# Two attentions of a three-block transformer kernel: when the first two output weight units are split, where the first maximum stands, and thirteen filler products

## The chip, the cores and the metric

The kernel runs on one core of one Trainium2 chip. The metric is the device time of one execution in microseconds. All times below are microseconds unless a column says ns. PE is TensorE (matrix products; PEld is its weight load), ACT is ScalarE, DVE is VectorE, POOL is GpSimd, SP the queue that issues most transfers.

## The reference

A sequence of 256 tokens of width 1024 goes through a first block (a recurrent mixer, a sparse attention, a feed-forward network) and a second block of two layers. Only the attentions of the second block are touched:

```
for layer in range(2):
    h = rmsnorm(x, attn_norm[layer])
    x = x + (even_mixer if layer == 0 else mla_mixer)(h)
    h = rmsnorm(x, ffn_norm[layer])
    x = x + (silu(h @ w_gate) * (h @ w_up)) @ w_down
even_mixer: 8 heads of stick-breaking attention (two sigmoids, a running product)
            and 8 heads of sliding-window softmax, concatenated, @ w_out
mla_mixer:  low-rank q, k, v for 16 heads, causal softmax, @ w_o
```

## The kernel before, in words

All weights stream through a ring of four slots, `ring`, in units of 1 MB (128 rows of 2048 floats). SP loads a unit when `unit_done` says that the unit four before it is used up. For the second block each unit is split before use: ACT writes `w_hi` (the high part) in two halves (`high_p`, line 1434, and `high_d`, line 1439), DVE writes `w_lo` (the rest) in two halves (`first_half`, line 1979, and `second_half`, line 1985), and PE makes three products for one: high by high, high by low, low by high. `w_hi` and `w_lo` hold two units, so a unit can be split once the unit two before it has been used.

Both attentions run through `heads_pipeline` on PE, as 19 steps s = 0 to 18, one head entering at each of the first 16. In step s PE makes the scores of head s (even attention: lines 1217 to 1221; MLA, the second: 1330 and 1331) into `ps[s % 2]`; then some products that are left over from the projections (`early`, as many as `rate` says, up to step 4; the even attention's last two query units, MLA's last value unit `mla_uv` and last query unit `mla_uq3`); from step 6 on a piece of the output projection (`fill`, `out_rows`, line 594); three transposes of the weights of head s - 2 (line 695); another piece of the output projection; and the product of head s - 3 with its values (lines 706 and 707). Pieces of the output projection go in the order of the contraction: the first 8 need output unit 0, the next 8 unit 1, and so on, so unit 0 is wanted at step 6 and unit 1 at step 10.

ACT, DVE and PE each have a fixed order of instructions, and a wait holds up all that stands behind it on the same engine. The order per step is: on ACT the nonlinearity of head s (even heads 0 to 7: sigmoids, lines 1795 and 1796; else the exponentials, 1450 and 1452, and the scaling of head s - 1, 1461 and 1462), the copy of the transposed weights `pT` (1804, the even attention's heads 0 to 7 only), in even steps from 4 on the high part of a pair of heads (`out_high`, 1468), then `out_weights`. On DVE: for head s the running product (2509, 2515) or the maximum (`softmax_max`, 2005 to 2012), the reciprocal of the sum of head s - 1, the copy of `pT` (2027, where ACT does not make it), in even steps from 4 on the low part of a pair (`out_low`, 2032), then `out_weights`. `ps[3]` takes the values of two heads; PE starts the next pair only after `out_low` has read it (`att_lo`). Steps 3 and 4 (MLA: 3 and 5) also take queries (1787 and 2497; 2576).

In MLA PE runs 13 products whose result nobody reads into `ps[3]` at the end of the early products of step 2 (`mla_idle`, `idle_products`, line 483). DVE splits `mla_uq3` (unit 8 of "mla") and then takes the first maximum.

Of the kernel before, what the change touches and what calls it, by code (L numbers as in the profile page):

```python
# [21 lines left out]
P = 128  # L22
# [5 lines left out]
H = D // HD  # L28
# [19 lines left out]
KEYS = P + S  # L48
# [8 lines left out]
U = {}  # L57
# [35 lines left out]
def build(nc, ins, out):  # L93
    weights, aux_d, const_d, small_d, rows_d, swbias_d, x_d, pos_d = ins
    with ExitStack() as ctx:
# [368 lines left out]
        def _(pe):  # L464
# [15 lines left out]
            def idle_products(n, bank, rows=oT_r):  # L480

                for _ in range(n):
                    pe.matmul(bank[:], rows[:, 0, 0:P], flat(rows[:])[:, 0:512], start=True, stop=True)
# [189 lines left out]
                            yield  # L673
                pe.drain().then_inc(unit_done, 1)

            def heads_pipeline(t0, scores, bank_free, p_ready_of, values, fill, early, rate, idle=None):

                for s in range(H + 3):
                    t = t0 + s
                    if s < H:  # L680
                        if s >= 2:
                            bank_free(s - 2)
                        scores(s, ps[s % 2]).then_inc(a_scores, 1)
                    for _ in range(rate.get(s, 0)):
                        next(early)
                    if idle:
                        idle(s)
                    if s >= 6:
                        next(fill, None)
                    if 2 <= s < H + 2:  # L690
                        p_ready_of(s - 2)
                        if s >= 3:
                            pe.wait_ge(a_pt, t - 2)
                        for kt in range(3):
                            m = pe.transpose(ps[2][:, kt * P:(kt + 1) * P], probs[(s - 2) % 3][:, kt * P:(kt + 1) * P],  # L695
                                             ident)
                        m.then_inc(a_t, 1)
                    if s >= 6:
                        next(fill, None)
                    if s >= 3:  # L700
                        h = s - 3
                        pe.wait_ge(a_pt, t0 + h + 1)
                        if h % 2 == 0 and t0 + h >= 2:
                            pe.wait_ge(att_lo, (t0 + h) // 2)
                        o = ps[3][h % 2 * HD:(h % 2 + 1) * HD, 0:S]
                        pe.matmul(o, values(h, 0), pT[:, h % 2, 0:S], start=True, stop=False)  # L706
                        m = pe.matmul(o[:, P:S], values(h, 1), pT[:, h % 2, S:KEYS], start=False, stop=True)
                        if h % 2:
                            m.then_inc(a_o, 1)
                for _ in fill:  # L710
                    pass
# [525 lines left out]
                    return va[:, kt, s * HD:(s + 1) * HD]  # L1237
                return vb[:, kt, (s - SB_HEADS) // 4 * HD:((s - SB_HEADS) // 4 + 1) * HD]

            def mla_idle(s):  # L1240

                if s == 2:
                    pe.wait_ge(kv_out, 5)
                    idle_products(13, ps[3])

            heads_pipeline(0, even_scores, even_bank_free, even_p, even_values, out_rows("even_out", 0),
                           even_queries(), {0: 1, 1: 1, 2: 3, 3: 2, 4: 1})
            normed(2)
# [84 lines left out]
            def mla_values(h, kt):  # L1333
# [4 lines left out]

            heads_pipeline(H, mla_scores, lambda h: pe.wait_ge(a_max, SW_HEADS + h + 1),
                           lambda h: pe.wait_ge(a_p, SW_HEADS + h + 1), mla_values, out_rows("mla_out", KT),  # L1340
                           late_units(), {0: 2, 1: 1, 2: 1, 3: 1, 4: 1}, mla_idle)
            normed(4)
            ffn_up(U["up2"], 2)
            ffn_down(2)
# [3 lines left out]
        def _(act):  # L1348
# [118 lines left out]
                act.wait_ge(a_o, p + 1)  # L1467
                act.activation(h_hi[:, p % KT, :], ps[3][:, 0:S], ACT.Copy).then_inc(att_hi, 1)

            def out_weights(u0, s, s0=0):  # L1470

                if s in (s0, s0 + 1):
                    act.wait_ge(unit_done, u0)
                    split_unit(u0, s - s0)
                if s in (10, 14):
                    act.wait_ge(unit_done, u0 + s // 4 - 1)
                    high_p(u0, s // 4)
                if s in (11, 15):
                    high_d(u0, s // 4)
# [310 lines left out]
            for s in range(H + 3):  # L1790
                if s < SB_HEADS:
                    act.wait_ge(a_scores, s + 1)
                    if s >= 2:
                        act.wait_ge(a_w, s - 1)
                    act.activation(beta[s % 2], ps[s % 2][:, 0:KEYS], ACT.Sigmoid)
                    act.activation(rest[s % 2], ps[s % 2][:, 0:KEYS], ACT.Sigmoid, scale=-1.0).then_inc(a_sig, 1)
                elif s < H:
                    h = s - SB_HEADS
                    softmax_exp(h, s % 3, sink=small("sinks")[:, h:h + 1])
                if SB_HEADS < s <= H:  # L1800
                    softmax_scale(s - 1 - SB_HEADS, (s - 1) % 3)
                if 2 <= s < SB_HEADS + 2:
                    act.wait_ge(a_t, s - 1)
                    act.activation(pT[:, s % 2, :], ps[2][:, 0:KEYS], ACT.Copy).then_inc(a_pt, 1)
                if s in (3, 4):
                    take_even_query(s - 3)
                if s >= 3 and s % 2 == 0:
                    out_high((s - 4) // 2)
                out_weights(U["even_out"], s, 4)
            boundary(2, U["up1"], small("g_ffn2")[:, 0:KT])  # L1810
            ffn_silu(U["up1"], 1)
            boundary(3, U["mla_down"], small("g_attn2")[:, KT:2 * KT])
# [51 lines left out]
            for s in range(H + 3):  # L1864
                if s < H:
                    softmax_exp(SW_HEADS + s, s % 3)
                if s == 1:
                    act.wait_ge(m_mm, MLA_MM["v10"])
                    act.activation(vm[:, 0, 512:D], ps[4][:], ACT.Copy).then_inc(kv_out, 1)
                if 0 < s <= H:  # L1870
                    softmax_scale(SW_HEADS + s - 1, (s - 1) % 3)
                if s >= 3 and s % 2 == 0:
                    out_high(KT + (s - 4) // 2)
                out_weights(U["mla_out"], s, 4)
            boundary(4, U["up2"], small("g_ffn2")[:, KT:2 * KT])
            ffn_silu(U["up2"], 2)
            square_x(5)
# [3 lines left out]
        def _(dve):  # L1881
# [108 lines left out]
                first_half(u0, name, m, i)  # L1990
                second_half(u0, name, m, i)

            def out_weights(u0, name, s, s0=0):

                if s in (s0 + 1, s0 + 2):
                    split_unit(u0, name, s - s0 - 1)
                if s in (11, 15):
                    first_half(u0, name, s // 4)
                if s in (12, 16):
                    second_half(u0, name, s // 4 - 1)  # L2000
# [503 lines left out]
            for s in range(H + 3):  # L2504
                if s < SB_HEADS:
                    beta_s, rest_s, left_s, w_s = beta[s % 2], rest[s % 2], left[s % 2], probs[s % 3]
                    dve.wait_ge(a_sig, s + 1)
                    for a, b, o in ((0, P, 0), (P, KEYS, 1)):
                        dve.tensor_tensor_scan(left_s[:, a + o:b + o][:, ::-1], rest_s[:, a:b][:, ::-1],
                                               rest_s[:, a:b][:, ::-1], 1.0, ALU.mult, ALU.bypass)  # L2510
                    dve.drain()
                    if s >= 3:
                        dve.wait_ge(a_t, s - 2)
                    for a, b, o in ((0, P, 0), (P, KEYS, 1)):
                        m = dve.tensor_tensor(w_s[:, a:b], beta_s[:, a:b], left_s[:, a + o + 1:b + o + 1], ALU.mult)
                    m.then_inc(a_w, 1)
                elif s < H:
                    h = s - SB_HEADS
                    if h == 0:
                        dve.wait_ge(swb_in, 16)  # L2520
                    if h < 3:
                        dve.wait_ge(a_t, s - 2)
                    dve.wait_ge(a_scores, s + 1)
                    softmax_max(s % 3, ps[s % 2], swb[:, h, P:S], swb[:, h, :], sink=small("sinks")[:, h:h + 1])
                if SB_HEADS < s <= H:
                    softmax_sum(s - 1 - SB_HEADS, (s - 1) % 3, sink=True)
                if SB_HEADS + 2 <= s < H + 2:
                    take_pT(s - 2, s % 2)
                if s in (3, 4):
                    take_even_query(s - 3)  # L2530
                if s >= 3 and s % 2 == 0:
                    out_low((s - 4) // 2)
                out_weights(U["even_out"], "even_out", s, 4)
            first_half(U["up1"], "ffn1", 0)
            add_rows(2)
            boundary(2, U["up1"], "ffn1", small("g_ffn2")[:, 0:KT])
# [83 lines left out]
            take_queries(5, 2)  # L2620
            dve.wait_ge(m_mm, MLA_MM["v01"])
            dve.tensor_copy(vm[:, 1, 0:512], ps[2][:]).then_inc(qv_out, 1)
            split_unit(down, "mla", 8)
            for s in range(H + 3):
                if s < H:
                    dve.wait_ge(a_scores, H + s + 1)
                    softmax_max(s % 3, ps[s % 2], const("causal")[:, 0:P], const("causal")[:, P:KEYS])
                if 0 < s <= H:
                    softmax_sum(SW_HEADS + s - 1, (s - 1) % 3)
                if s == 1:  # L2630
# [5 lines left out]
                    take_pT(H + s - 2, s % 2)  # L2636
                if s >= 3 and s % 2 == 0:
                    out_low(KT + (s - 4) // 2)
                out_weights(U["mla_out"], "mla_out", s, 4)
            first_half(U["up2"], "ffn2", 0)  # L2640
            add_rows(4)
            boundary(4, U["up2"], "ffn2", small("g_ffn2")[:, KT:2 * KT])
# [371 lines left out]
```

## Time and profile before

| | |
|---|---|
| median of 3 runs | 1369.06 (1368.37 to 1369.26) |
| the profiled execution, its own time | 1370.71 |
| its span in the trace | 1368.9 |
| mean granted TensorE clock over the span | 0.992 of full |
| busy share PE, PEld, DVE, ACT, POOL | 96%, 85%, 65%, 48%, 17% |
| even attention, PE's first scores to its last values | 785.3 to 857.7 |
| MLA attention, the same | 1103.0 to 1166.6 |

A row of the timeline reads: start, duration, engine, line, operation, out<-in, shapes, count, and in brackets how long the engine sat idle before it and what ended that. Successive rows of one engine overlap by about 0.1, because an instruction starts before the record of the one ahead of it ends. A row of the windows gives the stretch, its length, busy time and count of instructions of each engine, the granted clock (1.00 is 2.4 GHz, 0.50 is 1.2 GHz), the DMA share and GB/s.

### The profile page before, as it was taken

What the parts mean: (1) busy time and instruction counts of PE and PEld (TensorE: products, weight loads), DVE (VectorE), ACT (ScalarE), POOL (GpSimd) and SP (SyncE); (2) the same over time, 40 slices, a digit from 0 to 9 for tenths busy, and PEclk for the clock granted to TensorE, in tenths of its full rate; (3) what the DMA queues carried; (4) which work ended last, traced back from release to release, by engine and by line L of the source; (5) the groups of instructions that cost most, each with busy time, mean ns of one, the idle gap of its engine ahead of it and who ended that gap; (6) DMA issues with size and microseconds to landing.
All of it is one profiled execution on the core that took longest, in us unless ns stands there. A gap on an engine that the chain in (4) does not pass through costs nothing.

```text
span 1368.9 us, 26511 instructions
## 1 busy us (share of the span) xinstructions
PE 1316.1 (96%) x10058; PEld 1164.8 (85%) x10058; DVE 887.6 (65%) x1718; ACT 654.1 (48%) x1242; POOL 237.0 (17%) x326
## 2 busy tenths in 40 slices
PE   7999999988979999999999989999999999999997
PEld 6899999888879987999988966788887976888886
DVE  6677777756755676788846456666645666666644
ACT  4344444434326645676635456544434476544433
POOL 0001332212324421232301000122200000111100
PEclk9999999999999999999999999999999999999999
DMA  7311211104511144445555421454555531355552
GB/s 311 124 63 68 90 63 63 63 32 154 185 62 63 49 152 170 155 184 184 184 189 199 167 80 62 151 187 184 184 184 184 173 136 62 142 189 189 186 186 92
DMA packets 26771, 189.90 MB, mean 139 GB/s; under 512 B 2960, under 2 KB 3088, under 8 KB 4400
## 3 DMA queue, kind: packets, MB, share of 16 engines
q1 hardware_dynamic: 25632, 182.55, 36.8%
q0 software_dynamic: 1040, 5.96, 1.4%
q8 instruction: 70, 1.15, 0.3%
q14 instruction: 29, 0.24, 0.1%
HBM read 186.40 MB, written 1.05 MB: 137 GB/s over the span
## 4 chain that ended last, share of the span: by engine, by line
PE 84%; DVE 7%; ACT 3%; issue 2%; DVEq 2%; DMA 1%; POOL 1%; POOLq 0%; ACTq 0%; SPq 0%
PE ps L594 35%; PE ps L622 12%; PE ps L540 11%; PE ps L624 6%; PE ps L857 5%; DVE ring_r L1966 1%; PE ps L706 1%; PE ps L695 1%; DMA ring<-in_weights 1%; PE ps L565 1%; PE ps L876 1%; PE ps L966 1%; PE ps L572 1%; PE ps L956 1%; PE ps L763 1%
## 5 line engine op out<-in xcount | busy, mean ns | idle before, releaser
L1434 ACT ACTIVATE w_hi<-ring 128x1024 fp32r<-128x1024 f32 x125 | 132.6, 1061 | 306.8 <-PE ps L594 163.1
L622 PE MATMUL ps<-h_both,w_hi 128*128 128x512 f32 x704 | 249.3, 399 | 0.3 <-DVE h_both L1949 0.3
L1979 DVE TENSOR_TENSOR w_lo<-ring,w_hi 128x1024 fp32r<-128x1024 f32 x125 | 155.2, 1242 | 132.9 <-ACT w_hi L1434 132.8
L624 PE MATMUL ps<-h_both,w_lo 128*128 128x256 f32 x704 | 197.7, 281 | 0.0
L594 PE MATMUL ps<-h_both,w_hi 128*128 128x256 f32 x1008 | 182.9, 284 | 0.6 <-DVE h_both L1949 0.6
L622 PEld LDWEIGHTS ps<-h_both,w_hi 128*128 128x128 f32 x704 | 132.3, 188 | 34.5 <-issue 1.2
L594 PEld LDWEIGHTS ps<-h_both,w_hi 128*128 128x128 f32 x1008 | 156.9, 192 | 3.5 <-issue 3.4
L1985 DVE TENSOR_TENSOR w_lo<-ring,w_hi 128x1024 fp32r<-128x1024 f32 x125 | 157.3, 1258 | 0.0
L540 PE MATMUL ps<-oT_r,ring_r 128*128 128x256 f32 x512 | 145.2, 284 | 0.0
L594 PE MATMUL ps<-h_both,w_lo 128*128 128x256 f32 x504 | 142.6, 283 | 0.0
L624 PEld LDWEIGHTS ps<-h_both,w_lo 128*128 128x128 f32 x704 | 133.0, 189 | 0.0
L1439 ACT ACTIVATE w_hi<-ring 128x1024 fp32r<-128x1024 f32 x125 | 130.8, 1046 | 0.0
L594 PE MATMUL ps<-w_hi,a_hi 128*128 128x512 f32 x272 | 106.2, 390 | 0.0
L2075 DVE TENSOR_REDUCE arena<-ps 128x256 f32<-128x512 f32 x88 | 56.7, 686 | 76.3 <-PE ps L624 76.3
L594 PE MATMUL ps<-w_hi,a_lo 128*128 128x512 f32 x272 | 105.8, 389 | 0.0
L594 PE MATMUL ps<-w_lo,a_hi 128*128 128x512 f32 x272 | 105.8, 389 | 0.0
L540 PEld LDWEIGHTS ps<-oT_r,ring_r 128*128 128x128 f32 x512 | 98.1, 192 | 0.0
L594 PEld LDWEIGHTS ps<-h_both,w_lo 128*128 128x128 f32 x504 | 96.6, 192 | 0.0
L2662 POOL CAST a_hi<-arena 128x256 f32 (+1 forms) x66 | 31.5, 477 | 301.9 <-DVE arena L2052 301.9
L594 PE MATMUL ps<-w_hi,h_both 128*128 128x512 f32 (+1 forms) x192 | 70.4, 407 | 6.0 <-DVE w_lo L1985 6.0
L857 PE MATMUL ps<-arena 64*64 64x64 f32 x2048 | 71.8, 220 | 1.1 <-DVE arena L2174 0.8
L857 PEld LDWEIGHTS ps<-arena 64*64 64x64 f32 x2048 | 64.1, 134 | 8.5 <-issue 1.0
(424 smaller groups left out, 2902.3 us busy)
## 6 DMA issues: line engine op xcount, KB each, us to landing
ring<-in_weights SPq DMA_DIRECT2D x170, 1024.0 KB, 4.8
arena<-in_aux POOLq DMA_DIRECT2D x1, 2112.0 KB, 12.6
grow<-in_rows POOLq DMA_DIRECT2D x3, 512.0 KB, 4.2
cst<-in_consts SPq DMA_DIRECT2D x1, 1497.5 KB, 15.3
x<-in_x SPq DMA_DIRECT2D x1, 1024.0 KB, 5.0
arena<-in_swbias POOLq DMA_DIRECT2D x1, 1024.0 KB, 6.9
arena<-arena POOLq DMA_DIRECT2D x1, 1024.0 KB, 9.3
out<-xn SPq DMA_DIRECT2D x4, 256.0 KB, 2.3
```

The lines of the kernel that those rows point to most:

```text
L540: mm = pe.matmul(dst, w[a][:, k, tile * P:(tile + 1) * P], rhs[b][:, k, :], start=k == 0 and a == b, stop=k == KT - 1 and a == 1)
L565: pe.matmul(bank[:, P:KEYS], q[:, P:S], keys(0, S), start=True, stop=True).then_inc(s_mm, 1)
L594: m = pe.matmul(dst, l[a], r[b], start=first and n == 0 and a == b, stop=last and n == len(pairs) - 1 and a == 1)
L622: pe.matmul(bank[:].rearrange("p (a t) -> p a t", a=2), hi, h_both[:, :, k, :], start=k == 0, stop=False)
L624: m = pe.matmul(bank[:, 0:S], lo, h_hi[:, k, :], start=False, stop=k == KT - 1)
L857: return pe.matmul(dst, lhs, rhs, start=True, stop=True)
L1434: act.activation(w_hi[:, half_of(u0, m), WH:], ring[:, (u0 + m) % RING, WH:], ACT.Copy).then_inc(w_hi_p, 1)
L1439: act.activation(w_hi[:, half_of(u0, m), 0:WH], ring[:, (u0 + m) % RING, 0:WH], ACT.Copy).then_inc(w_hi_d, 1)
L1979: dve.tensor_tensor(w_lo[:, half_of(u0, m), WH:], ring[:, (u0 + m) % RING, WH:], w_hi[:, half_of(u0, m), WH:].bitcast(F32), ALU.subtract). ...
L1985: dve.tensor_tensor(w_lo[:, half_of(u0, m), 0:WH], ring[:, (u0 + m) % RING, 0:WH], w_hi[:, half_of(u0, m), 0:WH].bitcast(F32), ALU.subtrac ...
L2075: ins = dve.tensor_reduce(uc[j % 2][:, tile, :], bank[:].rearrange("p (a t) -> p t a", a=2), AX, ALU.add)
L2662: pool.tensor_copy(a_hi[:, m, :], act_f[:, j % 2, :])
```

## The change

In both attentions ACT splits output unit 0 earlier: at the end of its step 3 in the even attention and 2 in MLA, instead of step 4; and unit 1 at the end of its step 6 instead of 5. DVE follows at the end of step 4 (even) or 3 (MLA) instead of 5 for unit 0, and of step 7 instead of 6 for unit 1. Unit 0 waits only for the unit before the last (`u0 - 1`), whose half of `w_hi` it takes. In MLA the first maximum on DVE moves ahead of the split of `mla_uq3`, and the 13 filler products and their wait on `kv_out` are gone.

```diff
@@ PE: heads_pipeline @@
-                    if idle:
-                        idle(s)
@@ PE, MLA @@
-            def mla_idle(s):
-
-                if s == 2:
-                    pe.wait_ge(kv_out, 5)
-                    idle_products(13, ps[3])
...
-                           late_units(), {0: 2, 1: 1, 2: 1, 3: 1, 4: 1}, mla_idle)
+                           late_units(), {0: 2, 1: 1, 2: 1, 3: 1, 4: 1})
@@ ACT @@
-            def out_weights(u0, s, s0=0):
-
-                if s in (s0, s0 + 1):
-                    act.wait_ge(unit_done, u0)
-                    split_unit(u0, s - s0)
+            def out_weights(u0, s, s0):
+
+                if s in (s0, 6):
+                    act.wait_ge(unit_done, u0 - 1 if s == s0 else u0)
+                    split_unit(u0, int(s > s0))
...
-                out_weights(U["even_out"], s, 4)
+                out_weights(U["even_out"], s, 3)
...
-                out_weights(U["mla_out"], s, 4)
+                out_weights(U["mla_out"], s, 2)
@@ DVE @@
-            def out_weights(u0, name, s, s0=0):
-
-                if s in (s0 + 1, s0 + 2):
-                    split_unit(u0, name, s - s0 - 1)
+            def out_weights(u0, name, s, s0):
+
+                if s in (s0 + 1, 7):
+                    split_unit(u0, name, int(s == 7))
...
-                out_weights(U["even_out"], "even_out", s, 4)
+                out_weights(U["even_out"], "even_out", s, 3)
...
+            def mla_max(s):
+
+                dve.wait_ge(a_scores, H + s + 1)
+                softmax_max(s % 3, ps[s % 2], const("causal")[:, 0:P], const("causal")[:, P:KEYS])
+
+            mla_max(0)
             split_unit(down, "mla", 8)
             for s in range(H + 3):
-                if s < H:
-                    dve.wait_ge(a_scores, H + s + 1)
-                    softmax_max(s % 3, ps[s % 2], const("causal")[:, 0:P], const("causal")[:, P:KEYS])
+                if 0 < s < H:
+                    mla_max(s)
...
-                out_weights(U["mla_out"], "mla_out", s, 4)
+                out_weights(U["mla_out"], "mla_out", s, 2)
```

## Rows read from the trace of the kernel before

**Rows 1.** The page: shares of the chain that ended last, and the ring's transfers.
```profile
PE 84%; DVE 7%; ACT 3%; issue 2%; DVEq 2%; DMA 1%; POOL 1%; POOLq 0%; ACTq 0%; SPq 0%
...
ring<-in_weights SPq DMA_DIRECT2D x170, 1024.0 KB, 4.8
```

**Rows 2.** Busy time by stretches: after the even wait, steady steps, the MLA wait.
```profile
813.00:817.30 4.30, 4.24 (x14) 2.78 (x14) 1.51 (x4) 0.49 (x1) 0.00 (x0) 0.60 0.00 0
817.30:846.50 29.20, 29.18 (x139) 18.67 (x138) 18.59 (x71) 18.64 (x59) 0.00 (x0) 1.00 0.20 73
...
1121.00:1125.00 4.00, 1.51 (x9) 0.92 (x7) 3.96 (x9) 4.00 (x9) 0.00 (x0) 1.00 0.33 135
```

**Rows 3.** Timeline of PE, even attention, steps 6 to 9.
```profile
808.26 0.44 PE L1219 MATMUL ps<-hT_r 128*128 128x384 f32 x1
...
813.06 0.62 PE L594 MATMUL ps<-w_hi,h_both 128*128 128x512 f32 x1 [3.51 <-DVE w_lo L1985]
...
817.29 0.44 PE L1219 MATMUL ps<-hT_r 128*128 128x384 f32 x1
...
821.23 0.48 PE L1217 MATMUL ps<-arena 64*128 64x128 f32 x2
...
826.45 0.49 PE L695 MATMUL ps<-cst,sc 128*128 128x128 f32 x3
```

**Rows 4.** Timeline of ACT, even attention, steps 3, 4 and 8.
```profile
801.49 0.58 ACT L1787 ACTIVATE arena<-ps 64x512 f32<-64x512 f32 x1
803.12 0.49 ACT L1795 ACTIVATE arena<-ps 128x384 f32<-128x384 f32 x1 [1.05 <-PE ps L1221]
...
806.21 1.05 ACT L1434 ACTIVATE w_hi<-ring 128x1024 fp32r<-128x1024 f32 x1
...
824.64 0.47 ACT L1804 ACTIVATE pT<-ps 128x384 f32<-128x384 f32 x1
```

**Rows 5.** Timeline of DVE, even attention, steps 4, 5 and 8.
```profile
804.02 1.01 DVE L2509 TENSOR_TENSOR_SCAN arena<-arena 128x128 f32<-128x128 f32 x2 [2.97 <-ACT arena L1796]
...
805.65 0.68 DVE L2497 TENSOR_SCALAR arena<-ps 64x512 f32<-64x512 f32 x1
...
811.74 1.22 DVE L1985 TENSOR_TENSOR w_lo<-ring,w_hi 128x1024 fp32r<-128x1024 f32 x1
...
822.33 0.29 DVE L2005 CUSTOM_DVE_ANT_0 b_st<-ps,arena 128x128 f32<-128x128 f32 x1 [0.20 <-PE ps L1218]
```

**Rows 6.** Timeline of PE, MLA: fillers, first transposes, scores of heads 6 to 9.
```profile
1109.88 3.14 PE L483 MATMUL ps<-oT_r 128*128 128x512 f32 x13
1112.86 0.49 PE L695 MATMUL ps<-cst,sc 128*128 128x128 f32 x3
...
1121.28 0.49 PE L1330 MATMUL ps<-arena 128*128 128x128 f32 x2
...
1127.37 0.49 PE L1330 MATMUL ps<-arena 128*128 128x128 f32 x2
...
1130.74 0.49 PE L1330 MATMUL ps<-arena 128*128 128x128 f32 x2
...
1135.12 0.49 PE L1330 MATMUL ps<-arena 128*128 128x128 f32 x2
```

**Rows 7.** Timeline of ACT, MLA: scaling of head 0, exponential and `out_high` of step 4.
```profile
1109.87 0.50 ACT L1462 ACTIVATE sc<-sc,am 128x256 f32<-128x256 f32 x1
...
1118.01 0.40 ACT L1450 ACTIVATE sc<-sc,am 128x128 f32<-128x128 f32 x1 [1.37 <-DVE am L2012]
...
1119.59 0.36 ACT L1468 ACTIVATE h_both<-ps 128x256 fp32r<-128x256 f32 x1
```

**Rows 8.** Timeline of DVE, MLA: `mla_uq3`, head 1's `pT`, maximum 4, `out_low`.
```profile
1103.84 1.22 DVE L1979 TENSOR_TENSOR w_lo<-ring,w_hi 128x1024 fp32r<-128x1024 f32 x1
...
1115.50 0.55 DVE L2027 COPY pT<-ps 128x384 f32<-128x384 f32 x1
...
1117.09 0.29 DVE L2005 CUSTOM_DVE_ANT_0 sc<-ps,cst 128x128 f32<-128x128 f32 x1 [1.04 <-PE ps L1331]
...
1119.98 0.42 DVE L2032 TENSOR_TENSOR h_both<-ps,h_both 128x256 fp32r<-128x256 f32 x1 [0.95 <-ACT h_both L1468]
```

More of the change, by code:

```diff
@@ L674, in out_rows, with heads_pipeline @@
                 pe.drain().then_inc(unit_done, 1)
-            def heads_pipeline(t0, scores, bank_free, p_ready_of, values, fill, early, rate, idle=None):
+            def heads_pipeline(t0, scores, bank_free, p_ready_of, values, fill, early, rate):
                 for s in range(H + 3):
```

## The prediction, made before the change was built

> **What bounds the kernel now.** I read the page first: the chain that ended last runs 84% of its length over PE, so time is won only where PE waits, runs at the lower clock, or does work that nobody needs [rows 1]. Then PE's timeline in both attentions, for idle times in brackets. The even attention has one: 3.51 before the first piece of the output projection, in step 6, ended by DVE's low half of output unit 0 [rows 3, 5]. The stretch behind that wait has a granted clock of 0.60, the steady steps after it 1.00 [rows 2]. MLA has 13 filler products of 2.98 (1109.88 to 1112.86) [rows 6], and a wait for unit 0 that leaves PE only 1.51 busy of the 4.00 from 1121 on, with the clock still 1.00 [rows 2]. In step 8 it loses another 1.01 (1130.74 to 1135.12 is 4.38, where the step before took 3.37 [rows 6]), because unit 1's split on DVE, at the end of step 6, stands ahead of the next maximum. Last I read ACT and DVE around these places, to carry each moved instruction forward through its engine's queue.
>
> **Even attention, unit 0.** On ACT the split moves in behind the take of the queries, which starts at 801.49 and lets the next instruction start about 0.48 later. Its two halves (1.05 each, overlapping by 0.1 [rows 4]) hold ACT for 1.9, to 803.85. The sigmoids of head 4 are queued behind it; they started at 803.12 and now start 0.73 late, and so does DVE's running product: 804.75 for 804.02 [rows 4, 5]. DVE then needs 1.63 to its take of queries (804.02 to 805.65 [rows 5]), 0.6 for that, and 0.35 for `out_low`, which is no longer kept waiting: it is at the split by 807.3. Two halves of 1.22, overlapping by 0.1, are done at 809.65, and PE starts at 809.75 (0.1 after the end, as 813.06 follows 811.74 + 1.22 [rows 3, 5]). PE was ready 3.51 before 813.06, at 809.55. So 3.51 of waiting becomes 0.2. Nothing else in step 6 is later: ACT now has no split in steps 4 and 5, so `pT` of heads 2 and 3 is in time.
>
> The clock: step 6 took 9.03 (808.26 to 817.29); step 7, the same work without wait and at the full clock, took 3.94 (to 821.23) [rows 3]. If the wait is 0.2 and the clock holds, step 6 takes 4.15. **Gain 4.9**: 3.3 of waiting and 1.6 of half clock. Step 7 starts at 812.4, step 8 at 816.35.
>
> **Even attention, unit 1.** ACT comes to it at the end of step 6, behind `out_high`, which needs PE's values of head 3, done at about 812.5. `out_high` 0.3, the split 1.9: the sigmoids of head 7 start at 814.7, 0.9 later (803.12 to 804.02) the product of head 7 on DVE, 1.63 later the split there, at 817.2, and 2.3 later the maximum of head 8, at 819.5. That is 3.15 after step 8 starts, where before it was 1.10 (822.33 less 821.23). What waits for it is ACT: the exponential of head 8, then, behind it in the queue, `pT` of head 6, then PE's transposes in step 9. Before, that copy was over at 825.11 and the transposes stood at 826.45, a slack of 1.34 [rows 3, 4]. 2.05 more lateness leaves a new wait of 0.7. DVE's next maximum stands behind `out_low`, which waits for ACT behind the same copy, so step 10 waits again; between 0 and 0.7 more, and I take 0.5, since less than one step's slack is recovered. From step 10 on no `pT` is ACT's and both engines were busy 18.6 of 29.2 in steady steps [rows 2]; it recovers. **Cost 1.2, even attention 3.7 in all**; with neither wait 4.9, with 0.7 at each of three steps 2.8.
>
> **MLA, the fillers.** The transposes of head 0 stand behind them at 1112.86; the scaling that they need ended at 1110.37 (1109.87 + 0.50) [rows 6, 7]. So they start at 1110.43: **2.4 of the 2.98 are won**, the rest becomes waiting.
>
> **MLA, the first maximum.** It jumps a split of 2.3 that starts at 1103.84 [rows 8]; the split ends 0.85 later. The first exponential can start earlier, but the scaling of head 0 stands in ACT's queue behind the exponential of head 1, whose scores don't move, so this brings nothing. The late split may hold PE's first product with `mla_uq3` by some 0.2, ahead of the wait at 1110.4 that swallows it. **Nothing either way**; without that cover it costs 0.2.
>
> **MLA, unit 0.** On ACT it stands after the scaling of head 1, on DVE after `pT` of head 1. That copy followed the first transposes by 2.64 (1115.50 less 1112.86), so now it is at 1113.07; the split runs from 1113.5 to 1115.8 and the maximum of head 4 is queued behind it. From there it is a chain: 0.92 to the exponential (1117.09 to 1118.01), 1.58 to `out_high` (to 1119.59), 0.39 to `out_low` (to 1119.98), 0.42 for that, and 0.88 from its end (1120.40) to step 6 (1121.28) [rows 6 to 8]. 1115.8 + 4.19 is 1120.0. So of the 2.4 only 1.3 is left at the start of step 6: the split has become a wait of about 1.1 in step 5, for the weights of head 3 and then for `out_low`. But unit 0 is ready at 1115.9, so the wait in step 6 is gone: before, step 6 took 6.09 (to 1127.37); now 3.37 [rows 6], and a wait for the weights of head 4, whose maximum follows `out_low` on DVE, which I put at 0.3, between 0 and the 1.01 that step 8 shows. Step 7 starts at 1123.65, 3.7 earlier than before.
>
> **MLA, unit 1.** DVE now splits it at the end of step 7, ACT at the end of step 6. In step 8 the maximum then starts about 0.4 after its scores are there, and less than the 1.0 to 1.5 of slack is used. The 1.01 of step 8 is gone and none comes in its place: **MLA 4.7 in all**. If the same wait only moves one step on, 3.7.
>
> **The sum.** 3.7 + 4.7 is 8.4; the spread of the small waits speaks for a little less, 8.3. The profiled execution took 1370.71, its span 1368.9, so I expect 1362.4 for such a one and a span of 1360.6. The median of the runs is 1369.06, 1.65 below the profiled time; from it **1360.8**, 0.6% faster. What follows an attention is started by PE's own progress: units land in 4.8 once asked for, and nothing has a time of its own, so the gain should pass to the end whole.
>
> **Rivals.** *The clock falls after the fillers are gone.* The row that bears on it is the even attention's: 3.51 of idling, then 0.60; against it MLA's stretch with 2.49 of PE idle at 1.00 [rows 2, 3]. The new waits in steps 2 and 5 of MLA are 0.3 and 1.1 in two parts, in steps with little other work. A fall costs what it cost in step 6, 1.6, since half clock doubles the products until it rises; one gives 1362.4, two 1364. The Trainium skill has the rule against this edit ("TensorE: Matmul & The Clock Gate", Part 1): "the default state is throttled, and activity releases the throttle", so products nobody reads have a use. By that rule the removal costs up to 1.6 if the waits left behind count as idleness; by the rows it costs nothing. It agrees with the row of 0.60. I give it 0.16.
>
> *The side engines become the bound* (the other sign). The loop maximum, exponential, scaling, `out_high`, `out_low`, maximum could be longer than a PE step once a split has set it back, so that the wait comes back every step. There are 9 steps of the even attention and 13 of MLA behind the new waits; the time removed (4.9, 2.4, 2.5, 1.0) is 10.8, so it decides from 0.5 a step. At 0.7 a step it costs 15.4: 1373.7. For it: a split of 2.3 on DVE in a step of 3.4. Against: no more than 18.6 of 29.2 busy, and before no wait spreads past one step. 0.04.
>
> *It is taken back later.* The next stage could be bound by the weight stream, and PE would then wait there. Against: a transfer takes 4.8, four slots deep, and PE paces the requests [rows 1]. 1368.5 to 1369.5: 0.05.
>
> *Less waiting than I count*: neither new even wait nor MLA's 0.3. 1359.3: 0.10.
>
> **Numbers.** The likeliest, as summed: 0.65, its own range 1359.7 to 1362.3. For 8 in 10 I go from 1358.5 (no new wait anywhere, and MLA's 1.1 in step 5 smaller by most of itself) to 1364.9 (two falls of the clock, and one new wait more than I count). 0.2% of the time (2.7) is about what a measurement can tell from nothing. Faster by more than that, down to 1366.3: 0.65 + 0.10 + 0.16 = 0.91; within it 0.05; slower 0.04.
>
> **What would show it.** PE's first product with unit 0 at step 6 with less than 0.5 of idle in both; clock 1.00 through both attentions; waits of PE for `pT` by ACT in steps 9 and 10 of the even attention (0.7, 0.5); in MLA the first transposes 0.3 after the last early product, a wait of about 1 before the transposes of step 5, none in step 8. The prediction is wrong if unit 0 is still late at step 6, if the clock falls, or if PE waits in steps 11 and later.

## The result and the profile after

| | before | after |
|---|---|---|
| median of 5 runs each | 1369.1 (1368.37 to 1371.17) | 1360.87 (1359.23 to 1364.13) |
| the profiled execution, its own time | 1370.71 | 1363.63 |
| its span in the trace | 1368.9 | 1361.8 |
| PE, scores of head 0 to scores of head 11, even attention | 46.63 | 43.27 |
| PE, scores of head 0 to scores of head 10, MLA | 35.46 | 30.77 |
| PE, from the even stretch to MLA's | 271.10 | 271.29 |

The ratio after to before is 0.9944 (95% interval 0.9928 to 0.9959): 0.56% faster, forecast 0.6%. The three stretches are differences of starts in PE's timeline, each from the one profiled execution. Together the attentions gave 8.05 (3.36 and 4.69, forecast 3.7 and 4.7). The spans differ by 7.1: 0.78 was lost before the even attention and 0.19 between the two. Two single executions of the study ran far longer than all others, one of e8 (6702.57) and one of before beside e9 and e10 (2139.34), and are left out of the ratios. Line numbers of ACT, DVE and MLA are about 8 lower in the changed kernel (`high_p` is 1426, `first_half` 1971, `second_half` 1977, the maximum 1997, `out_low` 2024, ACT's `pT` 1796), those of PE's even scores and of its transposes 2 lower (1217, 693).

The page of the changed kernel, its chain and the ring's transfers, beside [rows 1]:

```profile
PE 82%; DVE 7%; ACT 4%; DMA 2%; issue 2%; DVEq 2%; POOL 1%; POOLq 0%; SPq 0%; ACTq 0%
...
ring<-in_weights SPq DMA_DIRECT2D x170, 1024.0 KB, 4.8
```

The path is PE's as before and a unit still lands in 4.8. The windows of the changed kernel: the even step 6 from its first product with unit 0 on, 29.2 of the even attention, and MLA's stretch in which unit 0 is wanted (columns as in [rows 2]):

```profile
810.60:813.30 2.70, 2.67 (x13) 1.79 (x13) 2.55 (x7) 1.27 (x3) 0.00 (x0) 1.00 0.00 0
813.00:842.20 29.20, 28.15 (x134) 17.69 (x132) 18.64 (x72) 18.76 (x54) 0.00 (x0) 1.00 0.15 51
1117.00:1121.00 4.00, 3.93 (x20) 2.50 (x19) 2.97 (x13) 3.14 (x12) 0.00 (x0) 1.00 0.14 59
```

The 0.60 behind the wait is now 1.00, and MLA's 1.51 of PE in 4.00 is 3.93. The second row has 1.05 without PE: that is the two new waits, and its DVE and ACT work (18.64, 18.76) is what the steady steps had before.

PE's timeline in the even attention, steps 5 to 10, beside [rows 3]:

```profile
808.41 0.62 PE L704 MATMUL ps<-pT,arena 128*64 128x256 f32 x2
...
809.17 0.44 PE L1217 MATMUL ps<-hT_r 128*128 128x384 f32 x1
...
810.63 0.47 PE L594 MATMUL ps<-w_hi,h_both 128*128 128x512 f32 x1 [0.17 <-issue]
...
813.32 0.44 PE L1217 MATMUL ps<-hT_r 128*128 128x384 f32 x1
...
817.25 0.49 PE L1215 MATMUL ps<-arena 64*128 64x128 f32 x2
...
823.31 0.52 PE L693 MATMUL ps<-cst,sc 128*128 128x128 f32 x3 [0.68 <-ACT pT L1796]
...
827.41 0.52 PE L693 MATMUL ps<-cst,b_st 128*128 128x128 f32 x3 [0.35 <-ACT pT L1796]
```

DVE and then ACT of the changed kernel in steps 4 to 9, beside [rows 4, 5]:

```profile
807.84 0.42 DVE L2024 TENSOR_TENSOR h_both<-ps,h_both 128x256 fp32r<-128x256 f32 x1
808.18 1.22 DVE L1971 TENSOR_TENSOR w_lo<-ring,w_hi 128x1024 fp32r<-128x1024 f32 x1
809.31 1.22 DVE L1977 TENSOR_TENSOR w_lo<-ring,w_hi 128x1024 fp32r<-128x1024 f32 x1
...
818.12 1.22 DVE L1971 TENSOR_TENSOR w_lo<-ring,w_hi 128x1024 fp32r<-128x1024 f32 x1
819.26 1.22 DVE L1977 TENSOR_TENSOR w_lo<-ring,w_hi 128x1024 fp32r<-128x1024 f32 x1
820.39 0.28 DVE L1997 CUSTOM_DVE_ANT_0 b_st<-ps,arena 128x128 f32<-128x128 f32 x1
```

```profile
803.66 1.05 ACT L1431 ACTIVATE w_hi<-ring 128x1024 fp32r<-128x1024 f32 x1
804.61 0.48 ACT L1787 ACTIVATE arena<-ps 128x384 f32<-128x384 f32 x1
...
814.65 1.05 ACT L1431 ACTIVATE w_hi<-ring 128x1024 fp32r<-128x1024 f32 x1
815.61 0.48 ACT L1787 ACTIVATE arena<-ps 128x384 f32<-128x384 f32 x1
...
821.62 0.40 ACT L1442 ACTIVATE b_st<-b_st,am 128x128 f32<-128x128 f32 x1 [3.47 <-DVE am L2004]
...
822.70 0.47 ACT L1796 ACTIVATE pT<-ps 128x384 f32<-128x384 f32 x1
```

How to read the three together: PE's transposes at 823.31 wait for the copy that starts at 822.70; the copy has no idle of its own, because it stands behind the exponential of head 8; the exponential waited 3.47 for the maximum that starts at 820.39; and the maximum stands behind DVE's two halves of unit 1. The bracket names ACT, but what ACT waited for is on DVE. ACT's own split of unit 1 (its second half at 814.65) has a share in it as well: it sets back the sigmoids of head 7 (815.61), and with them DVE's work on that head, behind which DVE's split stands. No run moves one of the two splits without the other.

PE's timeline in MLA, steps 2, 5 and the starts of steps 6 to 10, beside [rows 6]:

```profile
1108.03 0.55 PE L693 MATMUL ps<-cst,sc 128*128 128x128 f32 x3 [0.28 <-ACT sc L1454]
...
1116.11 0.55 PE L693 MATMUL ps<-cst,sc 128*128 128x128 f32 x3 [0.79 <-ACT sc L1454]
...
1116.88 0.62 PE L704 MATMUL ps<-pT,arena 128*64 128x256 f32 x2 [0.23 <-issue]
...
1117.65 0.49 PE L1322 MATMUL ps<-arena 128*128 128x128 f32 x2
...
1118.22 0.58 PE L594 MATMUL ps<-w_hi,h_both 128*128 128x512 f32 x1
...
1121.31 0.49 PE L1322 MATMUL ps<-arena 128*128 128x128 f32 x2
...
1124.67 0.49 PE L1322 MATMUL ps<-arena 128*128 128x128 f32 x2
...
1128.04 0.49 PE L1322 MATMUL ps<-arena 128*128 128x128 f32 x2
```

DVE in MLA, beside [rows 8]; ACT's last scaling before the transposes of step 5 (1115.57, 0.49) stands behind the exponential of head 4, which waited for this maximum:

```profile
1111.20 1.22 DVE L1971 TENSOR_TENSOR w_lo<-ring,w_hi 128x1024 fp32r<-128x1024 f32 x1
1112.33 1.22 DVE L1977 TENSOR_TENSOR w_lo<-ring,w_hi 128x1024 fp32r<-128x1024 f32 x1
1113.47 0.28 DVE L1997 CUSTOM_DVE_ANT_0 sc<-ps,cst 128x128 f32<-128x128 f32 x1
...
1116.36 0.42 DVE L2024 TENSOR_TENSOR h_both<-ps,h_both 128x256 fp32r<-128x256 f32 x1 [1.49 <-ACT h_both L1460]
```

The length of a step is the start of the scores of head s to that of head s + 1:

| step | before | forecast | after |
|---|---|---|---|
| even 5 | 2.49 | 2.49 | 2.66 |
| even 6 | 9.03 | 4.15 | 4.15 |
| even 9 | 3.57 | 4.27 | 4.43 |
| even 10 | 3.56 | 4.06 | 4.10 |
| MLA 1 | 1.72 | 1.72 | 1.82 |
| MLA 2 | 5.03 | 2.6 | 2.55 |
| MLA 5 | 2.11 | 3.2 | 3.25 |
| MLA 6 | 6.09 | 3.67 | 3.66 |
| MLA 8 | 4.38 | 3.37 | 3.37 |

The 0.78 lost ahead of the even attention arises in the first block, where both kernels have the same instructions. The same window in before and, second, in after:

```profile
384.00:388.00 4.00, 2.98 (x22) 2.67 (x22) 2.26 (x11) 0.30 (x1) 0.00 (x0) 1.00 0.00 0
```

```profile
384.00:388.00 4.00, 4.00 (x18) 3.73 (x17) 1.89 (x9) 0.30 (x1) 0.00 (x0) 0.52 0.00 0
```

Behind the same idle stretch the clock rose later in this execution (0.52 for 1.00). That belongs to the execution, not to the change: over the twelve profiles of this study the even attention starts anywhere between 782.87 and 787.20, with the same first block in all.

### The profile page after: what moved, and what is told of

Same layout as the page of the kernel before. It is cut to its first block, busy times and chain, and to the rows that moved or that the text cites. A ratio compares the mean times of both kernels' runs of the same rounds, so it can differ in the third digit from the quotient of the medians.

```text
span 1361.8 us, 26485 instructions
## 1 busy us (share of the span) xinstructions
PE 1313.5 (96%) x10045; PEld 1162.8 (85%) x10045; DVE 887.2 (65%) x1718; ACT 654.2 (48%) x1242; POOL 237.5 (17%) x326
## 3 DMA queue, kind: packets, MB, share of 16 engines
HBM read 186.40 MB, written 1.05 MB: 138 GB/s over the span
## 4 chain that ended last, share of the span: by engine, by line
PE 82%; DVE 7%; ACT 4%; DMA 2%; issue 2%; DVEq 2%; POOL 1%; POOLq 0%; SPq 0%; ACTq 0%
PE ps L594 34%; PE ps L622 12%; PE ps L540 11%; PE ps L624 6%; PE ps L855 5%; DMA ring<-in_weights 2%; DVE ring_r L1958 1%; PE ps L704 1%; PE ps L693 1%; PE ps L565 1%; ACT early_r L1349 1%; PE ps L874 1%; PE ps L572 1%; ACT xn L1393 1%; PE ps L964 1%
```

## The experiments

Single executions of one kernel spread widely (the 19 of before beside e1 to e4: 1364.92 to 1374.14), so terms of about 1 are read from the stretches of PE's timeline in the one profiled execution, and the time is given beside them. Stretch E is even heads 0 to 11, M is MLA heads 0 to 10, B the part between.

| run | E | M | B | median, ratio to before (95%) |
|---|---|---|---|---|
| before | 46.63 | 35.46 | 271.10 | |
| after | 43.27 | 30.77 | 271.29 | 1360.87, 0.9944 (0.9928 to 0.9959) |
| e1_even_only | 43.27 | 36.86 | 267.53 | 1363.19, 0.9960 (0.9943 to 0.9977) |
| e2_mla_only | 46.61 | 30.76 | 267.53 | 1360.95, 0.9942 (0.9920 to 0.9964) |
| e3_fillers_kept | 43.27 | 33.24 | 271.30 | 1361.80, 0.9945 (0.9923 to 0.9967) |
| e4_even_unit1_old_steps | 41.89 | 30.77 | 271.33 | 1358.83, 0.9920 (0.9898 to 0.9943) |
| e5_before_no_fillers | 46.60 | 33.07 | 267.51 | 1363.64, 0.9966 (0.9928 to 1.0004) |
| e6_first_max_back | 43.27 | 30.76 | 271.05 | 1360.86, 0.9955 (0.9928 to 0.9982) |
| e7_mla_unit1_old_steps | 43.28 | 34.61 | 269.02 | 1362.51, 0.9953 (0.9931 to 0.9974) |
| e8_before_fillers_in_even_step6 | 45.09 | 37.03 | 271.27 | 1369.54, 1.0008 (0.9990 to 1.0026) |
| e9_halves | 41.89 | 29.72 | 268.82 | 1358.03, 0.9923 (0.9902 to 0.9943) |
| e10_changed_again | 43.28 | 30.78 | 267.54 | 1358.81, 0.9927 (0.9904 to 0.9951) |

e1 to e4 share their runs of before (median 1369.23), so do e5 to e8 (1368.18), and e9 and e10 (1368.2).

Each E and M comes from one execution, but where the code is the same they repeat: E is 43.27 or 43.28 in six runs (after, e1, e3, e6, e7, e10), M is 30.76 to 30.78 in five (after, e2, e4, e6, e10). The times don't resolve the parts. By the medians e1 is 6.0 faster than before and e2 8.3, 14.3 together, where the whole change has 8.2 and the stretches say 3.36 and 4.70; e2's interval begins at 4.9, just above its 4.70, and e3, with the fillers put back, has the ratio of the changed kernel. The times that were expected were missed accordingly, all to the same side: e1 1363.19 for 1365.7, e2 1360.95 for 1364.4, e3 1361.80 for 1363.3, e4 1358.83 for 1359.5, e9 1358.03 for 1358.5. So what follows rests on the stretches. What B is made of is told in the last section.

**Even attention alone (e1).** The changed kernel with MLA as it was: fillers, first maximum and both split steps. Only ACT's weaker wait for unit 0 (`u0 - 1`) stays. `out_weights` takes the step of unit 1 as a last argument in e1, e2, e4, e7 and e9; the lines that put the fillers and the first maximum back are left out here (e3 and e6 show them).

```diff
...
-                if s in (s0, 6):
+                if s in (s0, s1):
...
-                out_weights(U["mla_out"], s, 2)
+                out_weights(U["mla_out"], s, 4, 5)
...
-                if s in (s0 + 1, 7):
-                    split_unit(u0, name, int(s == 7))
+                if s in (s0 + 1, s1):
+                    split_unit(u0, name, int(s == s1))
...
-                out_weights(U["mla_out"], "mla_out", s, 2)
+                out_weights(U["mla_out"], "mla_out", s, 4, 6)
```

> The change in the even attention alone; MLA keeps its fillers, its order and its old split steps. My theory: from the scores of head 0 to the scores of head 11 PE takes 43.3 (the changed kernel's time for it) instead of 46.6, with 0.2 of idle before the first piece of the output projection, clock 1.00, and waits in steps 9 and 10; MLA stays at 35.5 from the scores of head 0 to those of head 10. Time about 1365.7. Rival (the gain needs both parts, since the wait only moves): MLA or the stage between changes by more than 0.5.

E is 43.27, that of the changed kernel. M is 1.40 longer than before's, all of it in step 6 (7.51 for 6.09). The row of that wait in PE's timeline, first in before and then here, and the window that follows it here, show why:

```profile
1124.69 0.47 PE L594 MATMUL ps<-w_hi,h_both 128*128 128x512 f32 x1 [2.49 <-DVE w_lo L1985]
```

```profile
1115.33 0.77 PE L594 MATMUL ps<-w_hi,h_both 128*128 128x512 f32 x1 [2.49 <-DVE w_lo L1985]
```

```profile
1116.00:1120.00 4.00, 4.00 (x18) 2.78 (x16) 0.71 (x4) 2.06 (x7) 0.00 (x0) 0.70 0.00 0
```

The idle time is 2.49, to the hundredth that of before; here the clock fell behind it (the product takes 0.77 for 0.47), in before it did not [rows 2]. By its letter the rival is met, since M and B (3.57 shorter) both moved by more than 0.5; its mechanism isn't: no step of MLA but step 6 changed, its wait has the same length, and a B of 267.5 occurs in the unaltered changed kernel too (e10).

**MLA alone (e2).** The changed kernel with the even attention's split steps as they were.

```diff
-                out_weights(U["even_out"], s, 3)
+                out_weights(U["even_out"], s, 4, 5)
...
-                out_weights(U["even_out"], "even_out", s, 3)
+                out_weights(U["even_out"], "even_out", s, 4, 6)
```

> The change in MLA alone; the even attention as before. My theory: MLA takes 30.8 from the scores of head 0 to those of head 10 instead of 35.5, the even attention stays at 46.6 for heads 0 to 11 with its wait of 3.5 and the clock of 0.60 behind it. Time about 1364.4, so that the two parts add up to the whole change. Rival: they don't add up, by more than 0.5 in the two stretches.

E is 46.61 and M 30.76. In the stretches the two parts add up: 3.36 from e1's E and 4.70 from this M make 8.06, the changed kernel has 8.05. Neither part needs the other.

**The fillers put back (e3)** into the changed kernel.

```diff
...
+                if s == 2:
+                    pe.wait_ge(kv_out, 5)
+                    idle_products(13, ps[3])
...
```

> The changed kernel with the 13 filler products and their wait put back. My theory: PE's clock is 1.00 in MLA with and without them, so they only delay the transposes of head 0 and all behind them: the stretch from the scores of head 0 to those of head 10 grows from 30.8 to 33.2, time 1363.3. Rival (the fillers protect the clock): no more than 0.8 longer, or shorter.

M is 33.24: the fillers cost 2.47, all of it in step 2 (5.03 for 2.55). The other steps are as in the changed kernel, the waits of 0.79 and 0.23 in step 5 too, and the clock is 1.00 with and without them. They protect nothing here.

**Unit 1 of the even attention back in its old steps (e4)**, with unit 0 left early: ACT splits it in step 5, DVE in step 6.

```diff
-                if s in (s0, 6):
+                if s in (s0, s1):
...
-                out_weights(U["even_out"], s, 3)
+                out_weights(U["even_out"], s, 3, 5)
...
-                out_weights(U["even_out"], "even_out", s, 3)
+                out_weights(U["even_out"], "even_out", s, 3, 6)
```

> The changed kernel with unit 1 of the even attention split at its old steps (ACT 5, DVE 6), unit 0 early. My theory: the two waits of PE for ACT's copy in steps 9 and 10 come from DVE's split of unit 1 standing ahead of the maximum of head 8; at the old step that maximum is not late, both waits are gone, and heads 0 to 11 take 41.9 instead of 43.3. Time 1359.5, faster than the changed kernel by 1.4. Rival (a split anywhere here costs the same, the wait only moves to steps 7 or 8): 43.0 to 43.5.

E is 41.89: steps 9 and 10 are 3.57 each, and nothing else moved. So the late split of unit 1 (ACT's and DVE's together) is the whole cause of the 1.39 given back there, and that part of the change is a loss.

**The kernel before without its fillers (e5).**

```diff
-                           late_units(), {0: 2, 1: 1, 2: 1, 3: 1, 4: 1}, mla_idle)
+                           late_units(), {0: 2, 1: 1, 2: 1, 3: 1, 4: 1})
```

> The kernel before with nothing changed but the 13 fillers and their wait gone. My theory: the transposes of head 0 and the split steps behind them all move up together by 2.4, so MLA takes 33.0 from the scores of head 0 to those of head 10 instead of 35.5, and the wait for unit 0 in step 6 stays at about 2.5 (34.5 if the clock falls in it). Rival (unit 0 does not move up with PE, so the gain is given back at step 6): 35.0 to 35.5.

M is 33.07: 2.39 less, step 2 at 2.65. The wait of 2.49 in step 6 is still there and no clock fell behind it, without any fillers ahead. Its median is 4.5 below before's, more than the stretch gives, but from four executions, with an interval that reaches from 9.9 faster to nothing. In the profiled one B was 3.59 shorter than in before, which is no work of this edit (last section).

**The first maximum back behind the split of `mla_uq3` (e6).**

```diff
-            mla_max(0)
             split_unit(down, "mla", 8)
             for s in range(H + 3):
-                if 0 < s < H:
+                if s < H:
                     mla_max(s)
```

> The changed kernel with the first maximum of MLA behind the split of mla_uq3 again. My theory: it is worth nothing, since the scaling of head 0 waits behind the exponential of head 1 either way: MLA takes 30.6 to 30.8 (30.8 in the changed kernel), and PE's 0.1 at the first product with mla_uq3 is gone. Rival (the early maximum is what lets the transposes of head 0 start at once without fillers): 31.3 or more.

M is 30.76 for 30.77. Steps 1 and 2 are 1.71 and 2.66 for 1.82 and 2.55: the same 4.37. The early maximum is worth nothing, and the late split costs 0.1 that the wait behind it takes up.

**Unit 1 of MLA back in its old steps (e7)**, the same edit as e4's on the two `mla_out` lines.

> The changed kernel with MLA's unit 1 split at its old steps (ACT 5, DVE 6). My theory: the wait of 1.0 in step 8 comes from DVE's split standing ahead of the maximum of head 7, so it comes back: MLA takes 31.7 to 31.8 instead of 30.8. Rival (it came from being late after the wait for unit 0): 30.8.

M is 34.61, far above the 31.7 to 31.8 that I expected. ACT, DVE and PE of this run, each from its timeline, and the window behind the wait:

```profile
1115.78 1.04 ACT L1426 ACTIVATE w_hi<-ring 128x1024 fp32r<-128x1024 f32 x1
...
1119.24 0.36 ACT L1460 ACTIVATE h_both<-ps 128x256 fp32r<-128x256 f32 x1
```

```profile
1119.97 1.22 DVE L1971 TENSOR_TENSOR w_lo<-ring,w_hi 128x1024 fp32r<-128x1024 f32 x1
...
1122.24 0.28 DVE L1997 CUSTOM_DVE_ANT_0 sc<-ps,cst 128x128 f32<-128x128 f32 x1
```

```profile
1124.89 0.55 PE L693 MATMUL ps<-cst,sc 128*128 128x128 f32 x3 [1.92 <-ACT sc L1454]
```

```profile
1126.00:1129.00 3.00, 3.00 (x10) 2.05 (x10) 0.45 (x2) 0.79 (x3) 0.00 (x0) 0.54 0.00 0
```

The place was right, a late maximum ahead of the transposes of step 8, but the wait is 1.92 and not 1.0. With unit 0 early, both splits of unit 1 lie close behind step 5's wait: ACT's holds the exponential of head 6 and `out_high` back to 1119.24, with them DVE's `out_low` and split, and so the maximum to 1122.24. On top the clock fell to 0.54 behind the wait. Steps 7 to 9 took 3.47, 6.06 and 4.42 for 3.36, 3.37 and 3.37, which is 3.85: compared start by start with the changed kernel, PE is 2.25 late when it comes to the values of head 5 (1126.07; 0.11 of that is from step 7), and loses the other 1.60 from there to step 10, in which the clock is down. That both splits lie close together here is read from these rows; no run tests why the same steps cost 1.01 in before and 2.25 here. So in MLA the later step of unit 1 is the right one, in the even attention the wrong one.

**The kernel before with thirteen fillers in the even step 6 (e8)**, into a bank that nobody uses, in place of the idle time.

```diff
-                           even_queries(), {0: 1, 1: 1, 2: 3, 3: 2, 4: 1})
+                           even_queries(), {0: 1, 1: 1, 2: 3, 3: 2, 4: 1},
+                           lambda s: idle_products(13, ps[4]) if s == 6 else None)
```

> The kernel before with 13 filler products, whose result nobody reads, in the even attention ahead of the first piece of the output projection (step 6), in the time in which PE waits for unit 0 anyway. My theory: of the 4.9 that step 6 lost, 1.6 was the clock: with PE busy it stays at 1.00 and step 6 takes 7.4 instead of 9.0. Rival (the lower clock comes from something else than the idleness): 9.0, with a clock of 0.60 behind it.

PE's timeline of this run at unit 0:

```profile
808.07 3.24 PE L483 MATMUL ps<-oT_r 128*128 128x512 f32 x13
811.66 0.47 PE L594 MATMUL ps<-w_hi,h_both 128*128 128x512 f32 x1 [0.35 <-issue]
```

Unit 0 is as late as before, but the clock holds: step 6 is 7.50 for 9.03. That puts the clock's part of step 6 at 1.5 and leaves 3.35 (7.50 less 4.15) to the waiting, where the prediction had 1.6 and 3.3. The time shows none of it (1369.54, before 1368.18). In the profiled execution the clock fell in MLA (step 6 there 7.67 for 6.09), which took back 1.6; whether it did so in the others isn't known.

**Both terms mended (e9).** The even attention of e4, and in MLA DVE's split of unit 0 in two parts: the first half at the end of step 3, the second in step 4 between `pT` and `out_low`.

```diff
...
+                if s == 4:
+                    second_half(U["mla_out"], "mla_out", 0)
                 if s >= 3 and s % 2 == 0:
                     out_low(KT + (s - 4) // 2)
-                out_weights(U["mla_out"], "mla_out", s, 2)
+                if s == 3:
+                    first_half(U["mla_out"], "mla_out", 0)
+                if s != 3:
+                    out_weights(U["mla_out"], "mla_out", s, 2)
```

> The changed kernel with unit 1 of the even attention at its old steps (as e4) and, in MLA, DVE's split of unit 0 in two places: its first half at the end of step 3, its second half in step 4 behind the copy of head 2's weights and ahead of out_low. My theory: the wait of 1.1 in step 5 comes from the whole split standing ahead of the maximum of head 4; with half of it there the maximum is not late, the second half lies in DVE's wait for out_high, and MLA takes 29.7 from the scores of head 0 to those of head 10 instead of 30.8; the even attention 41.9. Time about 1358.5. Rival (the wait in step 5 is ACT's, whose split in step 2 makes the exponential of head 3 late): 30.6 to 30.8.

E is 41.89, M 29.72. DVE of this run around step 5:

```profile
1106.15 1.21 DVE L1971 TENSOR_TENSOR w_lo<-ring,w_hi 128x1024 fp32r<-128x1024 f32 x1
1107.29 0.28 DVE L1997 CUSTOM_DVE_ANT_0 sc<-ps,cst 128x128 f32<-128x128 f32 x1
...
1109.14 1.21 DVE L1977 TENSOR_TENSOR w_lo<-ring,w_hi 128x1024 fp32r<-128x1024 f32 x1
1110.27 0.42 DVE L2024 TENSOR_TENSOR h_both<-ps,h_both 128x256 fp32r<-128x256 f32 x1
```

Here the maximum of head 4 (1107.29) stands between the halves instead of behind both, `out_low` starts without a wait, and step 5 takes 2.20 for 3.25. Step 6 is 3.67 as before this edit: unit 0 is still in time. By the stretches this is the best version of the study: they are 2.43 below those of the changed kernel (1.38 even, 1.05 MLA). The medians, 1358.03 and 1358.81 for the changed kernel run on the same chip, can't show that much apart: the intervals overlap.

**The changed kernel again (e10)**, unaltered.

> The changed kernel itself, once more on another day of the same series, for a second profile. My theory: the stretches in the two attentions are the same to 0.1 (43.3 and 30.8), and what differs between executions lies outside them: where the clock falls in the first block, and the pace of the feed-forward stages (267.5 or 271.3 from the even attention's head 11 to MLA's head 0). Rival (the attentions vary themselves): a stretch that differs by more than 0.5.

E and M repeat to 0.01, while B differs by 3.75. What varies between these two executions of the changed kernel lies outside the attentions; where a wait of 2.49 is left in MLA, M varies too (e1, e8).

## Why the prediction was right, point by point

- **Even unit 0.** Right. The sigmoids of head 4 start at 804.61; with the 0.78 by which this execution is late everywhere, 803.83 (forecast 803.85), the split ends at 809.75 (809.65), and step 6 has the length forecast to the hundredth. e8 shows its two parts. One small thing was missing: PE's values of head 2 in step 5 come at 808.41, behind `out_low`, which is late by the edit (807.84 plus 0.42). I had followed `out_low` only as far as the split behind it on DVE, not to PE, which waits for `att_lo`. Step 5 is 0.17 longer for it, and step 7 starts 0.13 later than forecast (813.32 less 0.78 is 812.54, for 812.41).
- **Even unit 1.** Right in mechanism, place and releaser, a little small: 1.39 for 1.2. The maximum of head 8 starts 3.14 after step 8 (820.39 less 817.25; forecast 3.15). I took 0.7 from a slack of 1.34 between rows, and step 9 grew by 0.86. Not all of the 1.34 was slack: PE starts 0.14 after the end of the copy (822.70 plus 0.47, to 823.31). The recorded idle is 0.68, and the same goes for step 10 (0.53 longer, 0.35 recorded): a row's duration reaches about 0.16 past the start of the next, so the idle in brackets is that much less than the time lost. Whoever sums lost time takes differences of starts.
- **MLA.** Right term by term (table above). 2.4 for the fillers measured 2.48 in step 2, 2.39 alone in e5 and 2.47 in e3. The first maximum is worth nothing (e6). Unit 0 became a wait of 1.14 in step 5, forecast 1.1, and e9 shows its cause: DVE's whole split ahead of the maximum of head 4. Step 8 gave its 1.01 back.
- **The clock rival** (0.16). The profiled executions have no fall in either attention of the changed kernel, of e3, e4, e6, e9 and e10, nor in e2's MLA and e1's even attention. Its mechanism is real: e7 left a wait of 1.92 behind, and there the clock fell, at a cost of 1.60 where 1.6 was forecast. The waits that the change itself leaves behind are at most 0.79, and behind none of those did it fall. The Trainium skill's rule ("TensorE: Matmul & The Clock Gate", Part 1), that the array is throttled unless it is active, agrees with the row of 0.54. What the prediction drew from it, that products nobody reads have a use, depends on where they stand: in MLA's step 2 they only cost time (e3, e5), while in an idle time of 3.5 that exists anyway they kept the clock at 1.00 and saved 1.5 (e8). A short recorded idle is no assurance either: the last section has a fall behind one of 0.59, ahead of MLA.
- **Side engines as the bound** (0.04): steps 11 and later are 3.57, 3.56 and 3.56 as before, no wait spreads. **Taken back later** (0.05): from MLA's head 10 to the end is 230.4 in both. **Less waiting than I count** (0.10): the waits are there.
- **The sum.** 8.05 for 8.4 as summed (8.3 as taken): MLA is met, the even attention is short by 0.34, from 0.19 more in its new waits and 0.17 in step 5. The median fell by 8.2 and so met 1360.8 more closely than the mechanism alone earned, which is luck: the profiled executions differ by 7.08, and what lies outside the attentions moves by several us from execution to execution. The forecast left one thing out that the runs show: a wait of 2.49 in MLA's step 6 costs another 1.4 to 1.6 of half clock in some executions (e1, e8), and the change removes that too.

## What to carry to other kernels

Follow a moved block of work through the queue of each engine it stands in, forward to what the busiest engine waits for next: here the two large waits that were given back (1.39 and 1.14) had a split of 2.3 on DVE standing ahead of a maximum of 0.3, and in MLA cutting the split in two around the short, urgent instruction removed the wait (e9). Move each unit on its own: unit 1 wants its old step in the even attention and its new one in MLA, and only runs of one part at a time show that. Where executions spread by more than the term in question, compare the stretch of the timeline that the edit touches, start to start, and let the time confirm only the sum.

## What the runs showed of the hardware that was not expected

**The same wait, with and without a fall of the clock.** MLA's 2.49 of idle in step 6 is in before, e1, e5 and e8, with the same instructions around it. In before and e5 the granted clock stayed 1.00, in e1 and e8 it fell (step 6 is 6.09, 6.09, 7.51, 7.67). The even wait of 3.51 was followed by a fall each time (9.03, 9.03, 9.04 in before, e2 and e5). In before and e5, where the clock fell at the even wait, it held in MLA; in e1 and e8, where it held in the even attention, it fell in MLA. Four profiles can't tell whether that is chance. So one profile in which a wait of this length leaves the clock alone doesn't price the wait.

**A fall of the clock ahead of MLA, behind a recorded idle of 0.59.** B takes 267.5 in e1, e2, e5 and e10, 268.8 and 269.0 in e9 and e7, and 271.0 to 271.3 in the other six. Part of that is the clock, some 20 ahead of MLA's first scores. In every run PE makes 20 small products there (128x2) and then idles for a recorded 0.59. PE's timeline in before, and then its first product behind the idle time in e1:

```profile
1080.55 2.29 PE L1286 MATMUL ps<-cst,arena 128*128 128x2 f32 x20
1083.43 0.58 PE L594 MATMUL ps<-a_hi,w_hi 128*128 128x256 f32 x1 [0.59 <-DVE w_lo L1985]
```

```profile
1075.31 0.39 PE L594 MATMUL ps<-a_hi,w_hi 128*128 128x256 f32 x1 [0.59 <-DVE w_lo L1985]
```

In before the granted clock of 1083 to 1087 is 0.59, in e1 that of 1075 to 1079 is 1.00. It fell there in before, after, e3, e4, e6, e7, e8 and e9, and held in e1, e2, e5 and e10. By B of e9 and e7 less that of e10, whose products run at the same pace, a fall costs 1.3 to 1.5. In the attentions the clock never fell behind a recorded idle of 0.68 or 0.79 between full-size products. So the length of the recorded idle alone doesn't tell whether the clock is at risk; the row ahead of it must be read too.

**Two paces of the same products at a granted clock of 1.00.** The rest, 2.0 to 2.5, is the pace of the feed-forward products. PE's line 622 by groups from 929 to 941, in before and in e1:

```profile
L622 PE MATMUL ps<-h_both,w_hi 128*128 128x512 f32 x35 | 12.4, 399 | 0.0
```

```profile
L622 PE MATMUL ps<-h_both,w_hi 128*128 128x512 f32 x36 | 12.5, 394 | 0.0
```

Both stretches have no idle time and a clock of 1.00, yet a product is recorded with 399 ns in one and 394 in the other; 18 pairs of lines 622 and 624 take 6.36 (929.74 to 936.10) in before and 6.24 (929.78 to 936.02) in e1. The mean is 399 in before, after, e3, e4, e6 and e8, and 391 or 394 in e1, e2, e5, e7, e9 and e10. It is not the change: the changed kernel has both (after, and e10). What sets the pace is open; no run here was made to tell it.
